# A hybrid trunk on one core: three reorderings, in the load queues, at the turn between the layers, and ahead of a product

## The reference

```python
for i in range(DEPTH):
    xn = rmsnorm(h, pre_g[i])
    y = conv_gmlp_mixer(xn, ...) if i % 2 == 0 else mlstm_mixer(xn, ...)
    h = h + rmsnorm(y, post_g[i])
    gate = jax.nn.sigmoid(rmsnorm(h, ple_g[i]) @ w_ple_gate[i])
    h = h + gate * (p[i] @ w_ple[i])
```

## Time and profile before

| | |
|---|---|
| median of 3 runs | 985.06 us (983.53 to 986.02) |
| the profiled execution | 984.25 us, span 982.5 us |
| TensorE (PE) busy | 968.9 us, 99% |
| DVE, ACT, POOL busy | 671.0, 524.7, 99.5 us |
| granted TensorE clock, mean | 0.997 of full speed |
| DMA | 163.50 MB, mean 166 GB/s |

### The profile page before, as it was taken

How to read it: one execution, slowest core, us unless ns; L and a number is a source line. 1 busy time by engine, 2 the same in 40 slices (tenths; PEclk the granted TensorE clock), 3 DMA queues, 4 the chain that set the end, 5 groups by cost and what they waited for, 6 DMA issues and landing times.

```text
span 982.5 us, 12064 instructions
## 1 busy us (share of the span) xinstructions
PE 968.9 (99%) x4486; PEld 798.0 (81%) x4486; DVE 671.0 (68%) x885; ACT 524.7 (53%) x839; POOL 99.5 (10%) x136
## 2 busy tenths in 40 slices
PE   8999999999999989999999999999999999999998
PEld 7888888888877867887878888888888888888887
DVE  6767787786878749649797756775576676421745
ACT  6444545555555546636665656556653774441732
POOL 2020100101000104103010101010101000000400
PEclk9999999999999999999999999999999999999999
DMA  9654946749477974554946647392938163242122
GB/s 337 200 155 145 262 154 184 193 143 264 129 214 202 249 183 138 209 141 116 317 157 182 165 135 187 114 230 89 249 120 211 23 171 129 86 171 86 43 86 87
DMA packets 26781, 163.50 MB, mean 166 GB/s; under 512 B 3298, under 2 KB 4706, under 8 KB 8931
## 3 DMA queue, kind: packets, MB, share of 16 engines
q1 hardware_dynamic: 19234, 108.20, 28.9%
q0 software_dynamic: 7488, 54.53, 28.5%
HBM read 158.53 MB, written 4.19 MB: 166 GB/s over the span
## 4 chain that ended last, share of the span: by engine, by line
PE 88%; DMA 5%; DVE 3%; ACT 2%; issue 1%; POOL 0%; DVEq 0%; ACTq 0%
PE bank L2432 17%; PE bank L2435 17%; PE bank L2434 16%; PE bank L2338 6%; PE bank L2340 6%; PE bank L2339 6%; DMA raw<-in_slots 5%; DVE w_lo L1581 2%; PE bank L2491 1%; PE bank L2489 1%; PE bank L2490 1%; PE bank L2763 1%; PE bank L2465 1%; PE bank L2468 1%; PE bank L2467 1%
## 5 line engine op out<-in xcount | busy, mean ns | idle before, releaser
L1581 DVE TENSOR_TENSOR w_lo<-raw,w_hi 128x1024 fp32r<-128x1024 f32 x230 | 271.4, 1221 | 160.6 <-ACT w_hi L882 159.4
L2432 PE MATMUL bank<-w_hi,l_hi 128*128 128x512 f32 x784 | 316.9, 404 | 1.3 <-issue 0.9
L2435 PE MATMUL bank<-w_hi,l_lo 128*128 128x512 f32 x784 | 306.0, 390 | 0.0
L2434 PE MATMUL bank<-w_lo,l_hi 128*128 128x512 f32 x784 | 305.5, 390 | 0.0
L882 ACT ACTIVATE w_hi<-raw 128x1024 fp32r<-128x1024 f32 x230 | 230.7, 1054 | 116.3 <-DMA raw<-in_slots 62.6
L2432 PEld LDWEIGHTS bank<-w_hi,l_hi 128*128 128x128 f32 x784 | 147.3, 188 | 35.2 <-issue 2.9
L2435 PEld LDWEIGHTS bank<-w_hi,l_lo 128*128 128x128 f32 x784 | 147.2, 188 | 31.2
L2434 PEld LDWEIGHTS bank<-w_lo,l_hi 128*128 128x128 f32 x784 | 147.4, 188 | 30.3 <-issue 1.0
L708 POOL DMA_DIRECT2D raw<-in_slots x44 | 39.1, 970 | 466.1 <-DVE w_lo L1581 444.7
L1546 DVE TENSOR_TENSOR w_lo<-raw,w_hi 128x1024 fp32r<-128x1024 f32 x36 | 42.5, 1221 | 59.3 <-ACT w_hi L819 59.1
L819 ACT ACTIVATE w_hi<-raw 128x1024 fp32r<-128x1024 f32 x36 | 36.2, 1056 | 67.8 <-PE bank L2340 64.2
(11 more groups left out here) (267 smaller groups left out, 1341.6 us busy)
## 6 DMA issues: line engine op xcount, KB each, us to landing
raw<-in_slots SPq DMA_DIRECT2D x87, 1024.0 KB, 6.8
raw<-in_slots POOLq DMA_DIRECT2D x52, 1024.0 KB, 9.7
h<-in_x SPq DMA_DIRECT2D x8, 512.0 KB, 5.6
out<-h SPq DMA_DIRECT2D x4, 512.0 KB, 7.5
h<-out SPq DMA_DIRECT2D x4, 512.0 KB, 7.7
out<-h SPq DMA_DIRECT2D x7, 256.0 KB, 2.0
raw<-in_slots SPq DMA_DIRECT2D x2, 512.0 KB, 6.0
g_post<-in_g_rows SPq DMA_DIRECT2D x2, 512.0 KB, 4.7
```

Of the source, the lines that this page charges most:

```text
L1581: dve.tensor_tensor(w7_lo[:, ring(g), c], raw7[:, source(*STEPS[g]), c], w7_hi[:, ring(g), c].bitcast(F32), ALU.subtract).then_inc(w7_lo_r ...
L2432: pe.matmul(dst[:, :], left_hi, w7_hi[:, r, c], start=(first and k == 0), stop=False, skip_group_check=True)
L2434: pe.matmul(dst[:, :], left_hi, w7_lo[:, r, c], start=False, stop=False, skip_group_check=True)
L2435: done = pe.matmul(dst[:, :], left_lo, w7_hi[:, r, c], start=False, stop=(k == 3), skip_group_check=True)
```

## The change

SP: the load of B12 of half 1 moves ahead of the wait for the last mixing transposition; p's load moves ahead of those of h and the gate weights. POOL: sum 7 of half 0 moves ahead of the two sums for product 4. DVE at the turn: `normalise(5, 1, g_pre)` moves ahead of `gate(1, 2)`, and the second half of the split of TURN + 1 behind `left(1, 1, 0, 1)`. DVE ahead of (7,4): `s5_make(7, 0)` moves ahead of the split of TURN + 7, `s5_make(7, 1)` ahead of `gate_rows_end`.

```diff
@@ SP, out_fill @@
             sp.wait_ge(w7_lo_ready, split_done(OUT, 2))
             out_block(1, B21, BX, out_z_in)
+            sp.wait_ge(w7_lo_ready, split_done(OUT + 1, 2))
+            out_block(1, B12, BX, out_z_in)
             sp.wait_ge(ybt_ready, 8)
+            p_load(0)
             for t in range(TILES):
                 sp.dma_start(h[:, t], x[t * P:(t + 1) * P, :]).then_inc(h_in, 16)
             sp.dma_start(g_raw[:, :, :], gif_w).then_inc(gw_in, 16)
-            p_load(0)
-            sp.wait_ge(w7_lo_ready, split_done(OUT + 1, 2))
-            out_block(1, B12, BX, out_z_in)
             sp.wait_ge(tail_in, 16)
             sp.wait_ge(w7_lo_ready, split_done(OUT + 1, 3))
             load(0, wait=False)
@@ POOL, out_sums @@
             pool.wait_ge(out_z_in, 48)
             out_add(1, B22, BX, out_s7_in[1])
+            pool.wait_ge(w7_lo_ready, split_done(OUT, 3))
+            out_add(0, B12, BA, out_s7_in[0])
             for h, b in enumerate((BZ, BV)):
                 pool.wait_ge(w7_lo_ready, split_done(OUT + h, 6))
                 out_add(h, B21, b, out_s4_in)
-            pool.wait_ge(w7_lo_ready, split_done(OUT, 3))
-            out_add(0, B12, BA, out_s7_in[0])
@@ DVE, tail(0) @@
             gate(1, 0)
             lo7(TURN + 1, (0,))
             gate(1, 1)
-            lo7(TURN + 1, (1,))
             dve.wait_ge(g_pre_in, 16)
             normalise(4, 0, g_pre)
+            normalise(5, 1, g_pre)
             gate(1, 2)
-            normalise(5, 1, g_pre)
             left(1, 0, 0, 1)
             gate(1, 3)
             normalise(6, 2, g_pre)
             left(1, 0, 1, 2)
             left(1, 1, 0, 1)
+            lo7(TURN + 1, (1,))
             normalise(7, 3, g_pre)
@@ DVE, behind tail(0) @@
         lo7(TURN + 6)
         gate_rows()
+        s5_make(7, 0)
         lo7(TURN + 7)
+        s5_make(7, 1)
         gate_rows_end()
-        s5_make(7, 0)
-        s5_make(7, 1)
         lo7(TURN + 8)
         gate_sums()
```

## The result

The changed kernel takes 987.95 us (median of 14 runs, 986.65 to 989.78), the kernel before 985.9 us beside it (14 runs). The ratio on record is 1.0028, 95% interval 1.0020 to 1.0037: about 2.8 us slower (the two medians lie 2.05 us apart). The profiled execution took 987.21 us with a span of 985.5, against 984.25 and 982.5 before. Its busy times are those of before: 969.1 us for TensorE, 671.1 for DVE, 524.4 for ACT. Only POOL's fell, from 99.5 to 96.7. So again gaps and the clock decide.

The account below looks back on a forecast made before the run. TensorE, busy 99% of the span, was taken as the bound, so only its gaps and clock could change the time. +3.3, +1.8 and 0 gave +5.1 us on the profiled 984.25: 989.4 us, range 982 to 992.

Parts of the forecast that it names:

- Part 1: Output projection queues: the 3.1 us wait at (0,7) goes, one of about 6 us comes ahead of (0,4); +3.3 us.
- Part 2: Turn to the second layer: second transposition 1.5 us earlier, but the first product waits for ACT's left operand; +1.8 us.
- Part 3: Value combination ahead of (7,4): the 0.9 us wait goes, a new one comes at (8,3); 0, bounds -1.0 and 0.
- rival A: Sums for product 4 come late, but by less; all three parts cost less, in all 985.0 us; chance 0.25.
- The step from landing to product: Output projection: from the landing of the last sum 4 to the start of (0,4), 9.2 us.
- the 1.7 us of low clock: Behind the new wait ahead of (0,4), matmuls at the lower clock cost 1.7 us, as behind the old wait.
- SP's later start: Output projection: SP waits for the split of (1,2) first, so POOL's sum 7 of half 0 issues 1.4 us later.
- the contention of the gain rows: Output projection: SP's two gain rows run beside POOL's sums and delay their landing; 2.9 us, counted in full.
- the gain is given back: At (8,3): TensorE comes 1.0 us earlier but waits for DVE's combination, so the gain from (7,4) is lost.
- B: Rival: the waits at all three sites simply go and nothing takes their place; 976.9 us, chance 0.13.
- C: Rival: the low clock comes more than once, after the gap ahead of (0,3) and after the turn; 991.6 us, chance 0.12.

Follow-up runs that it names:

- e1: Kernel before with only the two queue reorderings of the output projection (SP's loads and POOL's sums): 985.62 us, ratio 1.0013.
- e9: Kernel before with only POOL's order changed, sum 7 of half 0 ahead of both sums for product 4: 985.79 us, ratio 1.0016.
- e8: e1 with one more edit, SP sends load(0) only after both sums for product 4 have landed: 980.63 us, ratio 0.9981 to the kernel before.
- e10: Kernel before with only normalise(5,1) moved ahead of gate(1,2), the half split left in place: 987.16 us, ratio 1.0032.
- e7: Kernel before with only the second half of the split of TURN + 1 moved behind left(1,1,0,1): 983.93 us, ratio 1.0000.
- e3: Kernel before with only the two moves of s5_make ahead of (7,4): 984.84 us, ratio 1.0009.
- e11: Changed kernel with load(0) on SP held until both sums for product 4 have landed, gain rows ahead of it: 983.31 us, ratio 0.9993 to the kernel before.
- e12: e8 with the half split of the turn moved behind left(1,1,0,1): 980.53 us, ratio 0.9966 to the kernel before.
- e4: Kernel before with only SP's order changed, B12 of half 1 ahead of h, p and the gate weights: 983.04 us, ratio 0.9989.
- e6: Kernel before with s5_make(7,0) behind gate_rows_end and the split of TURN + 7 behind that: 984.56 us, ratio 1.0008.
- e2: Kernel before with only the two moves at the turn, normalise(5,1) and the half split: 986.17 us, ratio 1.0020.
- e5: e4 with residual(0,0) on DVE moved behind both combinations d: 984.6 us, ratio 1.0010 to the kernel before.

## Why the prediction was right or wrong

The forecast was 989.4 us, the result 987.95, and of the profiled execution 987.2 against 989.4. The sign and the main mechanisms of parts 1 and 2 were right. The size of part 1 was too large and that of part 3 too small. The whole change cost 2 to 3 us (2.05 by the medians, 2.8 by the ratio, 2.96 by the traces) where 5.1 were forecast, so the direction is well founded and the size is not: rival A, at 985.0, lies as near to the profiled execution as the forecast does. By the bound that the prediction set itself (slower above 988.0) the result is a hair inside no change, while its interval, which is narrower than that bound, is clear of it.

- **Part 1, +3.3 forecast, +0.9 in the trace.** The wait moved from (0,7) to (0,4), and e1 and e9 show it is POOL's order. The step from landing to product, 9.2 us, and the 1.7 us of low clock came as computed. Two terms were too large, SP's later start and the contention of the gain rows. SP's later start was charged with 1.4 us and cost 0.3 at most (ACT had sum 6 of half 1 at 338.18, and before at 338.30; with the 0.46 us added by which this trace ran early there, that is 0.3 later). Why so little isn't shown by a run. SP itself did start later as forecast: 321.17, against 320.28 before, and 1.35 us later with the 0.46 added. So the group went out at 347.33 on the clock of the trace before, 1.1 us sooner than the 348.4 of the forecast. From issue to landing it was 22.35 us in place of 23.6, another 1.2 us; together 2.3 of the 2.4 us by which part 1 was mis-sized. That 22.35 came so near is in part luck, since errors in its terms cancel. e8, with load(0) away, shows 8.0 us for the first transfer (charged: 8.6) and 11.4 for the other two (charged: 9.5, from landings of transfers that had not gone out together). Load(0) cost 3.1 us (22.5 against 19.4; charged: 2.6). The gain rows, charged with 2.9, can have cost 0.5 at most in e8: they went out at 358.13, and up to 364, when the last sum's packets were through, SP's queue had taken 4.5% of 11 us. To count their engine time in full was the fault, since most of them was left when the last sum was through.
- **Part 2, +1.8 forecast, +2.0.** The order on ACT is the cause, as argued: square of gate(1,2), then the left operand. With the 0.46 us taken off by which the changed kernel came to the turn late, tile 1 is normalised from 448.47 (forecast 448.55) and the first product stands at 453.7, the number of the forecast. The rest of the sum came out by luck, for another reason than mine. I had DVE carry the chain to (7,5) with the half split on its back (+1.1 - 0.5). But TensorE did not wait at (7,5) at all. The clock fell behind the 2.8 us gap, which I had only in the bounds: from the first product to the third it took 1.1 us more (462.80 - 454.15 = 8.65 us, before 460.06 - 452.54 = 7.52), and the 0.28 us wait at (7,5) went. 1.15 + 1.1 - 0.3 = 2.0. Of the two moves the normalisation is the loss (e10), the half split is none (e7).
- **Part 3, 0 forecast, about +0.5.** The wait at (7,4) went and one of 0.9 came at (8,3), as written. The step that failed is "the gain is given back", and no more: I stopped the chain there. (DVE's wait for (7,7) was 1.17 us, forecast 0.6. That isn't what decides: in e3 it was 0.36, and both new waits came.) Behind it `s6_add(8)` on DVE is late by as much as DVE lags, SP's load, issued at 504.13 before, goes out at 507.06, ACT has its block at 527.21 in place of 524.26, and the state product waits 0.7 us. "The gain is given back 25 us later" should have been followed by: who else waits for DVE's later work. That this load is what holds the state back is read from the traces; no run took it away, and in e11, where the low clock held TensorE back at (8,3), the state product did not wait.
- **Rivals.** A had the size of part 1 about right (+0.3 there, +0.9 measured), with sums that come late but by less, and a part 2 and a part 3 that are too good. B needed the landing within 17.4 us of 348.4, or 18.5 of the 347.33 at which the group went out; the best of all runs is 19.35. Worked out as an estimate from the Trainium skill's figure ("DMA: Bandwidth & Descriptors", section "Anatomy of one DMA — SWDGE (gpsimd) path") three transfers would be there after some 9 us; this case's adding transfers are not of that kind: in e8 the queue moved 2.22 MB in 97.4% of 11 us, 207 GB/s, while SP's plain loads in e1 moved 1.16 MB in 26.9% of 11 us, 392 GB/s. C's second low clock did come, at the turn; the gap ahead of (0,3) was 1.08 us in place of 2.2, and the clock stayed at 1.00 behind it.

## What to carry to other kernels

When a queue's order is changed, price what is moved back as carefully as what is moved ahead, up to the last one of the group that a consumer waits for, and look for the plain load beside it: holding back a load that nobody needs yet was worth more here than either order. When a step moves ahead on one engine, follow the step it displaces onto the other engines, since a written order there (ACT's square ahead of the left operand) can make the displaced one the critical one. A local wait that goes is a gain only if the engine that caused it has slack until its next meeting with the bound engine; count that engine's work between the two meetings.

## What the runs showed of the hardware

- **Idle time and the clock.** TensorE's gaps of 1.70, 1.75, 1.85 and 2.41 us (e12, e8, e11 and e4, ahead of (0,4)) were followed by a granted clock of 1.00. Lower values followed these, of 0.50 to 0.80 in the 2 us behind the gap: 2.13, 2.60 and 2.71 us (e6, e2 and e3) and 3.07 to 4.16 ahead of (0,7), 2.78 and 2.79 at the turn, 2.92 in e5, and 4.70 to 4.87 ahead of (0,4). The shortest of them, in e6:

```profile
364.54 0.47 PE L2465 MATMUL bank<-w_hi,l_hi 128*128 128x512 f32 x1 [2.13 <-DVE w_lo L1581]
```

```profile
364.00:366.00 2.00, 1.46 (x4) 1.25 (x5) 2.00 (x3) 2.00 (x4) 0.00 (x0) 0.72 0.00 0
366.00:368.00 2.00, 2.00 (x6) 1.53 (x5) 2.00 (x3) 2.00 (x4) 0.00 (x0) 0.50 0.72 180
```

So a gap of 2.13 us had the low clock behind it and one of 2.41 had not. The 0.86 us gap of e11 was followed by 0.61 and 0.54, while the 0.88 us gaps at the same place in e3 and in the changed kernel were followed by 1.00. The length of one gap alone doesn't decide; I leave open what does. Shortening one from 4.9 to 1.75 us gave back 1.7 us more than its length.
- **An adding transfer costs the DMA engines nearly twice a plain load** of the same bytes (207 GB/s of the engines' time, against 392 for the plain loads in e1 and, worked out from the earlier trace rows, 357 for those from 321 to 330). Its landing, from the issue of a group of three to the last, repeats closely: 22.35, 22.4 and 22.5 us with load(0) beside it, 19.35, 19.4 and 19.5 without.
- **POOL beside DVE.** The power of 128x1 takes 1.51 us beside the half split, which reads two tiles of SBUF, and 0.56 without it (e10 against e7 and the changed kernel; the earlier trace rows for before). The Trainium skill ("GPSIMD Engine Reference", section "Specifications") says that POOL's SBUF interfaces are shared with VectorE, with contention where DVE has two SBUF inputs; the trace agrees.
